# Decoder block with HGRN2, dilated attention and 32 experts: value weights split into places of their own

## The reference

```
h    = rmsnorm(x) * norm1_g
proj = h @ w_in                     # 1024 x 3584: seven groups of 512 columns
q, f, v, g, aq, ak, av = split(proj)
f    = lb + (1 - lb) * sigmoid(f);  k = 1 - f
o_a  = hgrn2(q, k, v, log f)        # 4 heads of 128, gated linear recurrence in chunks
o_a  = head_rmsnorm(o_a) * hgrn_g * silu(g)
o_b  = head_rmsnorm(dilated_attention(aq, ak, av)) * attn_g   # 8 heads of 64
x    = x + concat(o_a, o_b) @ w_out
h2   = rmsnorm(x) * norm2_g
x    = x + moe(h2)                  # top 4 of 32 experts, clamped SwiGLU, two weight matrices each
out  = rmsnorm(x) * final_g
```

## Time and profile before

| | us |
|---|---|
| median of 3 runs | 1433.44 (1433.32 to 1434.06) |
| profiled execution | 1433.96 |
| its span | 1432.2 |
| TensorE busy | 1346.2 (94%) |
| VectorE busy | 1183.2 (83%) |
| ScalarE busy | 1060.7 (74%) |

### The profile page before, as it was taken

One profiled execution on the slowest core, in us unless ns is written; L12 is line 12 of the kernel. 1 busy time (PEld: TensorE's weight loads), 2 busy tenths in 40 slices (PEclk: granted clock), 3 DMA queues, 4 the chain that ended last, 5 costly groups with the idle time before them and its releaser, 6 DMA issues.

```text
span 1432.2 us, 19035 instructions
## 1 busy us (share of the span) xinstructions
PE 1346.2 (94%) x6385; PEld 1062.0 (74%) x6386; DVE 1183.2 (83%) x1048; ACT 1060.7 (74%) x895; POOL 270.3 (19%) x135
## 2 busy tenths in 40 slices
PE   6989999899899999999999999999999999999991
PEld 5778876558687777877777877777777777777771
DVE  4448645467899999999999999999999999999992
ACT  6345423335588989898988889898988889898962
POOL 0000000000123222313312122313222122223120
PEclk9999999998899999999999999999999999999996
DMA  8323235126599999999999999999999999999954
GB/s 237 110 59 89 60 115 238 74 104 248 217 366 401 421 400 413 413 410 412 409 409 400 414 395 414 405 409 406 411 406 402 402 398 420 391 414 406 421 176 147
DMA packets 71684, 459.82 MB, mean 321 GB/s; under 512 B 7301, under 2 KB 36005, under 8 KB 47008
## 3 DMA queue, kind: packets, MB, share of 16 engines
q1 hardware_dynamic: 64416, 438.12, 75.4%
q0 software_dynamic: 7232, 21.22, 6.2%
HBM read 443.35 MB, written 20.19 MB: 324 GB/s over the span
## 4 chain that ended last, share of the span: by engine, by line
PE 71%; DMA 16%; DVE 4%; ACT 4%; issue 3%; SPq 0%; POOL 0%; ACTq 0%; POOLq 0%; DVEq 0%
PE psum L1725 47%; DMA w_raw_pair<-w_up 14%; PE psum L1499 6%; PE psum L1496 3%; PE psum L1741 3%; PE psum L1718 2%; PE psum L1585 2%; PE psum L1708 1%; PE psum L1609 1%; PE psum L1627 1%; ACT lin L759 1%; DVE w_low L1182 1%; PE psum L1572 1%; ACT sig L760 1%; PE psum L1863 1%
## 5 line engine op out<-in xcount | busy, mean ns | idle before, releaser
L1182 DVE TENSOR_TENSOR w_low<-w_raw_pair,w_high 128x2048 fp32r<-128x2048 f32 x384 | 862.1, 2285 | 66.1 <-ACT w_high L726 65.4
L726 ACT ACTIVATE w_high<-w_raw_pair 128x2048 fp32r<-128x2048 f32 x384 | 722.4, 1913 | 117.6 <-PE psum L1725 50.5
L1725 PE MATMUL psum<-w_high,x_high 128*128 128x512 f32 x1024 | 276.2, 391 | 0.0
L1725 PE MATMUL psum<-w_low,x_high 128*128 128x512 f32 x1024 | 273.9, 389 | 0.0
L1725 PEld LDWEIGHTS psum<-w_low,x_high 128*128 128x128 f32 x1024 | 192.2, 188 | 40.3
L1725 PEld LDWEIGHTS psum<-w_high,x_high 128*128 128x128 f32 x1024 | 191.6, 188 | 40.4 <-issue 0.4
L556 POOL DMA_INDIRECT residual_rows<-y_rows,scatter_rows x32 | 147.3, 4604 | 368.3 <-ACT y_rows L765 368.3
L1725 PE MATMUL psum<-w_high,a_high 128*128 128x512 f32 x512 | 162.5, 399 | 0.0
L1725 PE MATMUL psum<-w_low,a_high 128*128 128x512 f32 x512 | 158.7, 391 | 0.0
L544 POOL COPY gather_rows<-row_t 128x1 int32 (+1 forms) x32 | 20.2, 630 | 723.7 <-DVE row_t L1343 356.6
L1725 PE MATMUL psum<-w_high,x_low 128*128 128x512 f32 x544 | 150.8, 399 | 0.5 <-DVE x_low L1348 0.5
(11 more groups left out here) (274 smaller groups left out, 1439.4 us busy)
## 6 DMA issues: line engine op xcount, KB each, us to landing
w_raw_pair<-w_up SPq DMA_DIRECT2D x128, 2048.0 KB, 15.3
w_raw_pair<-w_down SPq DMA_DIRECT2D x64, 2048.0 KB, 14.6
w_in_raw<-w_in SPq DMA_DIRECT2D x28, 512.0 KB, 3.8
w_buf<-w_out SPq DMA_DIRECT2D x2, 2048.0 KB, 11.1
x_rows<-x SPq DMA_DIRECT2D x4, 512.0 KB, 5.3
x_rows<-x SPq DMA_DIRECT2D x1, 2048.0 KB, 18.7
residual_rows<-x_rows SPq DMA_DIRECT2D x4, 512.0 KB, 2.7
normed_rows<-h_rows SPq DMA_DIRECT2D x4, 512.0 KB, 2.6
```

Source lines behind the costliest of these rows:

```text
L726: act.activation(wh[:, q.slot(m, SPL), :], raw[q.slot(m, RAW)][:, :], ACT.Copy).then_inc(wh_ready, 1)
L1182: dve.tensor_tensor(wl[q.slot(m, RAW)][:, :], raw[q.slot(m, RAW)][:, :], wh[:, q.slot(m, SPL), :].bitcast(F32), ALU.subtract).then_inc(wl_ ...
L1725: ins = pe.matmul(o[:, j, :], x_part, w_part[:, j * 512:(j + 1) * 512], start=(first and n == 0), stop=(last and n == len(passes) - 1))
```

## The change

1. **Value weights.** Columns 8 to 11 (v) are split into `w_v_high` and two halves of `w_v_low`, which lie over rows that attention and head outputs use later. Their `w_high` waits for no product; `w_low` is two subtractions of half a column. Columns 12 to 15 (g) take the places that q used. ScalarE splits column 8+j ahead of the copy of q j; columns 12 and 13 come ahead of the logarithms and 14 and 15 behind them, all ahead of the exponentials of head 0 and the copies of v.
2. **Row scales** are made for tiles 0 and 1 once their squares are summed, and for 2 and 3 after that. VectorE scales tiles 0, 1 and 3, ScalarE tile 2. TensorE turns tiles 0 and 1 for seven blocks, then the gains, then the eighth block, then tiles 3 and 2.
3. **Constants** come in two transfers: identity and ones at the old place, the rest behind weight columns 0 and 1, together with the router bias. VectorE waits for the rest before the scan of head 0; TensorE waits for the gains only where it turns them.
4. **VectorE's bias run** moves from behind `w_low(11)` to between `w_low(9)` and `w_low(10)`; `w_low(10..13)` follow it, then the scan, `w_low(14)` and `w_low(15)`, and the scaled operands.

```diff
+        WVH = over("w_v_high", [P, 4, DK, P], v0 + 8192, F32R)
+        WVL = [over("w_v_low_upper", [P, 4, DK // 2, P], v0 + 24576, F32R),
+               over("w_v_low_lower", [P, 4, DK // 2, P], hg0 + 38912, F32R)]
...
+        V_AT = 4 * GORDER.index("v")
...
-            sp.dma_start(C[:, :], consts).then_inc(S("c_in"), 16)
+            sp.dma_start(C[:, 0:2 * P], consts[:, 0:2 * P]).then_inc(S("c_in"), 16)
...
-            sp.dma_start(rb_rows[:, :], router_b.to_broadcast([P, NE])).then_inc(S("rb_in"), 16)
             for c in range(4 * len(GORDER)):
                 if c == 2:
+
+                    sp.dma_start(C[:, 2 * P:], consts[:, 2 * P:]).then_inc(S("c_rest"), 16)
+                    sp.dma_start(rb_rows[:, :], router_b.to_broadcast([P, NE])).then_inc(S("rb_in"), 16)
...
-            act.wait_ge(S("mean_eps"), 1)
-            root(act, r1, ss1)
-            for i in range(TT // 2):
-                act.wait_ge(S("r1"), 1)
-                act.activation(XN[:, i, :], X[:, i, :], ACT.Copy, scale=r1[:, i:i + 1]).then_inc(S("xn"), 1)
+                if i % 2:
+                    act.wait_ge(S("mean_eps"), i // 2 + 1)
+                    root(act, r1[:, i - 1:i + 1], ss1[:, i - 1:i + 1])
+            act.wait_ge(S("r1"), 2)
+            act.activation(XN[:, 2, :], X[:, 2, :], ACT.Copy, scale=r1[:, 2:3]).then_inc(S("xn_third"), 1)
 
             def w_high(c):
 
                 act.wait_ge(S(f"w_in{c % 2}"), 16 * (c // 2 + 1))
-                if c >= 4:
-                    used(act, c - 4)
-                act.activation(WPH[:, c % 4, :, :], WPR[:, c % 2, :, :], ACT.Copy).then_inc(S("w_in_high"), 1)
+                if V_AT <= c < V_AT + 4:
+                    dst = WVH[:, c - V_AT, :, :]
+                else:
+                    dst = WPH[:, c % 4, :, :]
+                    if c >= 4:
+                        used(act, c - 8 if c < V_AT + 8 and c >= V_AT else c - 4)
+                act.activation(dst, WPR[:, c % 2, :, :], ACT.Copy).then_inc(S("w_in_high"), 1)
...
             for h in range(HH):
+                w_high(8 + h)
                 full(act, "q", h)
                 act.activation(Q[:, h, :], bank("q", h), ACT.Copy).then_inc(free_sem("q", h), 1)
-                w_high(8 + h)
+            w_high(12)
+            w_high(13)
             for h in range(HH):
                 act.wait_ge(S("f_ready"), h + 1)
                 act.activation(F[:, h, :], F[:, h, :], ACT.Ln).then_inc(S("log_f"), 1)
+            w_high(14)
+            w_high(15)
             hgrn_exps(act, 0)
             for j in range(4):
                 full(act, "v", j)
                 act.activation(V[:, j, :], bank("v", j), ACT.Copy).then_inc(free_sem("v", j), 1)
-            for c in range(12, 16):
-                w_high(c)
...
+            dve.wait_ge(S("ss1"), 2)
+            row_scales(slice(0, 2))
+            dve.wait_ge(S("r1"), 1)
+            scaled_rows(0)
+            scaled_rows(1)
             dve.wait_ge(S("ss1"), TT)
-            mean_eps(ss1, ss1, D)
-            refined(r1, ss1, rtmp[:, 0:TT]).then_inc(S("r1"), 1)
-            dve.wait_ge(S("r1"), 1)
-            for i in range(TT // 2, TT):
-                dve.tensor_scalar(XN[:, i, :], X[:, i, :], r1[:, i:i + 1], None, ALU.mult).then_inc(S("xn_rest"), 1)
+            row_scales(slice(2, TT))
+            dve.wait_ge(S("r1"), 2)
+            scaled_rows(3)
...
                 dve.wait_ge(S("w_in_high"), c + 1)
-                dve.tensor_tensor(WPL[:, c % 4, :, :], WPR[:, c % 2, :, :], WPH[:, c % 4, :, :].bitcast(F32), ALU.subtract
-                                  ).then_inc(S("w_in_low"), 1)
+                if V_AT <= c < V_AT + 4:
+                    for n in range(2):
+                        k = slice(n * DK // 2, (n + 1) * DK // 2)
+                        ins = dve.tensor_tensor(WVL[n][:, c - V_AT, :, :], WPR[:, c % 2, k, :], WVH[:, c - V_AT, k, :].bitcast(F32),
+                                                ALU.subtract)
+                else:
+                    ins = dve.tensor_tensor(WPL[:, c % 4, :, :], WPR[:, c % 2, :, :], WPH[:, c % 4, :, :].bitcast(F32), ALU.subtract)
+                ins.then_inc(S("w_in_low"), 1)
...
-            for c in range(8, 12):
-                w_low(c)
+            w_low(8)
+            w_low(9)
             dve.wait_ge(S("bias_in"), 64)
...
             link(dve.memset(vals_t[:, :, :, :], 0.0))
+            for c in range(10, 14):
+                w_low(c)
...
+            dve.wait_ge(S("c_rest"), 16)
             decays(0)
+            w_low(14)
+            w_low(15)
             scaled(0)
-            for c in range(12, 16):
-                w_low(c)
...
             pe.wait_ge(S("c_in"), 16)
+            for i in range(2):
+                pe.wait_ge(S("xn"), i + 1)
+                for k in range(DK - 1):
+                    if i == 0:
+                        begin("hT", k)
+                    turned(k, i)
             pe.wait_ge(S("vec_in"), 80)
             pe.transpose(begin("vec")[:, 0:32], vec_rows[:, :], ident[0:32, 0:32]).then_inc(full_sem("vec"), 1)
+            begin("hT", DK - 1)
+            turned(DK - 1, 0)
+            turned(DK - 1, 1)
             for k in range(DK):
-                o = blocks("hT", k)
-                for i in range(TT):
...
+                pe.wait_ge(S("xn"), 3)
+                turned(k, 3)
+                pe.wait_ge(S("xn_third"), 1)
+                turned(k, 2).then_inc(full_sem("hT", k), 1)
```

More of the change, by code:

```diff
@@ L712, in _ @@
                 if h == AH - 1:
-                    act.wait_ge(S("mean_eps"), 2)
+                    act.wait_ge(S("mean_eps"), 3)
                     root(act, ra[:, 0:EARLY], ssa[:, 0:EARLY])
-            act.wait_ge(S("mean_eps"), 3)
+            act.wait_ge(S("mean_eps"), 4)
             root(act, ra[:, EARLY:], ssa[:, EARLY:])
@@ L833, in _ @@
                         router_half(i - 1, 1)
-                act.wait_ge(S("mean_eps"), 4 + i)
+                act.wait_ge(S("mean_eps"), 5 + i)
                 root(act, r2[:, i:i + 1], mean2[:, i:i + 1])
@@ L900, in _ @@
                 act.activation(YF[:, i, :], XF[:, i, :], ACT.Square, accum_out=ss1[:, i:i + 1]).then_inc(S("ssf"), 1)
-                act.wait_ge(S("mean_eps"), 4 + TT + i)
+                act.wait_ge(S("mean_eps"), 5 + TT + i)
                 root(act, r1[:, i:i + 1], ss1[:, i:i + 1])
@@ L930, in spread, with row_scales, scaled_rows @@
                 return col.unsqueeze(2).broadcast_to([P, col.shape[1], n])
-            dve.wait_ge(S("ss1"), TT)
-            mean_eps(ss1, ss1, D)
-            refined(r1, ss1, rtmp[:, 0:TT]).then_inc(S("r1"), 1)
-            dve.wait_ge(S("r1"), 1)
-            for i in range(TT // 2, TT):
-                dve.tensor_scalar(XN[:, i, :], X[:, i, :], r1[:, i:i + 1], None, ALU.mult).then_inc(S("xn_rest"), 1)
+            def row_scales(r):
+                mean_eps(ss1[:, r], ss1[:, r], D)
+                refined(r1[:, r], ss1[:, r], rtmp[:, r]).then_inc(S("r1"), 1)
+            def scaled_rows(i):
+                dve.tensor_scalar(XN[:, i, :], X[:, i, :], r1[:, i:i + 1], None, ALU.mult).then_inc(S("xn"), 1)
+            dve.wait_ge(S("ss1"), 2)
[3 more added lines that the diff above has]
+            scaled_rows(1)
+            dve.wait_ge(S("ss1"), TT)
+            row_scales(slice(2, TT))
+            dve.wait_ge(S("r1"), 2)
+            scaled_rows(3)
             full(dve, "vec")
@@ L1470, in blocks, with turned @@
                 return blocks_of(begin(*name))
+            def turned(k, i):
+                return pe.transpose(blocks_of(bank("hT", k))[:, i, :], XN[:, i, k * P:(k + 1) * P], ident)
             pe.wait_ge(S("c_in"), 16)
+            for i in range(2):
[4 more added lines that the diff above has]
+                    turned(k, i)
             pe.wait_ge(S("vec_in"), 80)
             pe.transpose(begin("vec")[:, 0:32], vec_rows[:, :], ident[0:32, 0:32]).then_inc(full_sem("vec"), 1)
+            begin("hT", DK - 1)
+            turned(DK - 1, 0)
+            turned(DK - 1, 1)
             for k in range(DK):
-                o = blocks("hT", k)
-                for i in range(TT):
[L1478 to L1482, removed]
-                ins.then_inc(full_sem("hT", k), 1)
+                pe.wait_ge(S("xn"), 3)
+                turned(k, 3)
+                pe.wait_ge(S("xn_third"), 1)
+                turned(k, 2).then_inc(full_sem("hT", k), 1)
             def project(g, j):
@@ L1494, in project @@
                     for h_part, w_part in ((HL, WPH), (HX, WPH), (HX, WPL)):
+                        if g == "v":
+                            w_rows = WVH[:, :, k, :] if w_part is WPH else WVL[k // (DK // 2)][:, :, k % (DK // 2), :]
+                        else:
+                            w_rows = w_part[:, :, k, :]
                         if rows:
-                            ins = pe.matmul(blocks_of(o), h_part[:, k, j * P:(j + 1) * P], w_part[:, :, k, :],
```

(1 more changed line is left out.)

## The result

| | before | changed |
|---|---|---|
| median, us | 1433.38 (1432.13 to 1434.06, 4 runs) | 1424.06 (1421.62 to 1424.38, 4 runs) |
| profiled execution, its span | 1433.96, 1432.2 | 1423.96, 1422.2 |

The ratio is 0.9926 (95% interval 0.9912 to 0.9939), so 8.7 to 12.6 us were won. Forecast were 1422.2 in a range of 1420 to 1427, and 11.5 us.

What follows compares the result with a forecast made beforehand. TensorE was taken to bound the first 200 us, the experts' weights on full DMA engines 400 to 1350 us. Terms 2.1 + 2.9 + 0.2 + 1.4 + 1.6 + 2.3 + 0.3 + 0.7 = 11.5 us gave 1422.2, range 1420 to 1427.

Steps and rivals of the forecast that it cites:

- The start: Before the first product of f: earlier constants, weight columns and row scales let f begin at 17.2, not 19.36; -2.1 us.
- That rival: Two bursts of transposes with a hole leave f's first products at the low clock; costs 1.4 us, 1423.6; chance 0.07.
- The hole at v: L1496, first value product waiting for its weights' split: own places remove the hole, -2.9 us, and 0.16 us of drain.
- the clock: Products of v: without the hole no drop to clock 0.50, so 22.0 us instead of 23.45; -1.4 us.
- Gate weights: Earlier splits of columns 12 to 15 remove waits at L1499 (1.6 us) and L1531 (2.3 us), and drain of 0.3.
- o_rows: L1556, head 0: VectorE has o_rows ready before TensorE asks, so the wait goes; -0.7 us.
- Sum: All steps together give 11.5 us: 1422.5 from the profiled execution, 1421.9 by the median; 1422.2 was said.
- That it reaches the end: Expert weight stream: its starts hang on TensorE, so an earlier mixer moves everything behind it; the opposing rival, 1433.4, had 0.04.

Runs made afterwards that it cites:

- the repetition: The changed kernel run once more with no edit; median 1423.76 us, ratio 0.9918.
- gate late: The changed kernel with weight columns 12 to 15 split at their old places on ScalarE and VectorE; 1428.46 us, ratio 0.9953.
- bias late: The changed kernel with VectorE's bias run back behind column 11, columns 12 and 13 behind it; 1423.44 us, ratio 0.9918.
- places only: The changed kernel with the start as before (constants in one transfer, row scales together); median 1424.90 us, ratio 0.9931.
- the constants alone: The kernel before with nothing but the constants in two transfers; first product of f at 19.68 us, o_rows at 122.50.
- hole-filled kernel: The kernel before with 12 extra matmuls in the hole between q and v; one timed run, 1436.29 us.
- the scales alone: The kernel before with nothing but the row scales in two pairs; first product of f at 19.14 us, o_rows at 120.55.
- the start alone: The kernel before with the changed constants, row scales and transposes, places and split order as before; 1433.21 us, ratio 0.9979.

## Why the prediction was right

By its own steps:

- *The start*, 2.1: where h_low came last, f began 7.78 us behind the last square in three traces (the repetition, gate late, bias late); 7.8 were forecast (17.2 - 9.40), and before it was 9.96. The step had TensorE done with the transposes ahead of h_low, at 0.175 us each. In the first trace of the changed kernel it wasn't: all 32 took 0.23, so that h_low was ready at 15.98 and f began at 16.52, at the low clock. That rival was right there and not in the repetition. It cost o_rows 0.8 us: 100.60 us from the last square, 99.77 in the repetition.
- *The hole at v*, 2.9 + 0.2, and *the clock*, 1.4: gone; v 21.76 instead of 23.45, 1.7. Column 11 was done at 58.3 (58.5 forecast), with q's end at 60.86 (60.9). The bias run waited for nothing, as said.
- *Gate weights*, 1.6 + 2.3 + 0.3, and o_rows, 0.7: gone. The scaled operands were done at 77.1 (77 forecast), the copy of the keys at 83.7 (84.3). Late order brought back 6.0, not 4.9: the step said nothing of a clock drop behind L1531, because the trace of before had none there.
- *Sum*, 11.5 at o_rows: 11.9, 11.6 and (places only) 9.6 for 9.4. That the first trace comes so near is in part luck: x gave it 1.0 us and the low clock took 0.8. Counted from the last square, the three gains are 10.9, 11.8 and 8.9 us. The mechanism doesn't hang on this: the holes that the steps name are gone from the waits.
- *That it reaches the end*: shown until fold 4 in the traces, with 11.2 of 11.9 us; the repetition's ratio gives 9.5 to 14.2 us. That the first median lay 1.9 us above the forecast is within what the expert stage scatters by; the forecast gave 0.5 us for that, and 3 would have been right.

What the prediction didn't see is that the two parts of the start are worth nothing one by one. As the sum took both together, that cost it nothing. Whether the start is worth less without the places stays open: in the traces it moved o_rows by 0.1 us without them and by 2.0 to 2.3 with them, but the timed runs give 1 to 5 us without them and, from the ratios 0.9931 and 0.9926 or 0.9918, some 1 to 2 us with them.

## What to carry to other kernels

Follow a hole to what its releaser waited for: here a split waited for its place, not for its data, and a place of its own removed the hole, the clock drop behind it and the lateness that head 0 inherited. Two things that end together hide each other: edits that give nothing alone (here constants and scales, by the begin of f) may be worth 2 us as a pair, so test the pair before dropping either. And size a mixer's gain on landmarks in the trace, counted from where x had landed, since here the stage behind it, with the DMA engines full, scattered by 3 us, as much as the longest hole was worth.

## What the runs showed of the hardware

- Whether the granted clock falls in a hole differed from hole to hole: it was 0.50 (1.2 of 2.4 GHz) behind holes of 2.9 (v), 2.8, 2.6 and 2.15 us, and stayed at 1.00 behind 1.6 (gate products). At the state products it stayed at 1.00 behind 2.3 us in the kernel before and behind 3.25 with the constants alone, and fell behind 2.3 in the hole-filled kernel. So in these traces the length of the hole alone doesn't tell. A drop cost 1.3 to 1.7 us.
- Transposes can be followed by faster ones with no other product between than that of the gains: with the scales alone, 14 took 3.25 us (0.23 each) and the next 18 took 2.19 (0.12 each), and so it was in the repetition of the changed kernel. In the first trace of the same kernel, and in that of the start alone, the 18 stayed at 0.23. The Trainium skill ("TensorE: Matmul & The Clock Gate", Part 4: PE-mode transpose) says that transposes don't count for the clock. The faster traces speak against it; the slower ones alone would not.
- In the first 16 us of all traces the clock's row reads 1.00, whether a transpose takes 0.23 or 0.12 us.
- x lands between 8.1 and 9.6 us (begin of the last square) over the fourteen traces, all of which load it first; where h_low comes last, f moves along.
